# Thirteen Strassen pairs in the down-projection instead of twelve, placed one position earlier, with the order of the low parts changed

## What is computed

```python
def conv_glu_ffn(u, w_up, conv_ffn, b_conv_ffn, w_down):
    h = causal_dwconv(u @ w_up, conv_ffn) + b_conv_ffn
    return (jax.nn.silu(h[..., :D_FF]) * h[..., D_FF:]) @ w_down      # D_FF = 5632, result 256 x 2048

def hybrid_layer(x, ...):
    z = rms_norm(x, g_mix) @ w_in
    ...
    x = x + merged @ w_out
    x = x + cross_attend(rms_norm(x, g_cross), rms_norm(mem, g_mem), ...)
    x = x + conv_glu_ffn(rms_norm(x, g_ffn), w_up, conv_ffn, b_conv_ffn, w_down)
```

## Time and profile before

| | us |
|---|---|
| median of 3 runs (1742.89 to 1744.5) | 1743.65 |
| the profiled execution | 1744.25 |
| its span, first to last instruction | 1742.5 |
| PE busy in the span | 1732.3 |
| DVE busy | 1184.1 |
| ACT busy | 956.1 |

### The profile page before, as it was taken

How to read it: one execution, slowest core, us unless ns; L and a number is a source line. 1 busy time by engine, 2 the same in 40 slices (tenths; PEclk the granted TensorE clock), 3 DMA queues, 4 the chain that set the end, 5 groups by cost and what they waited for, 6 DMA issues and landing times.

```text
span 1742.5 us, 25685 instructions
## 1 busy us (share of the span) xinstructions
PE 1732.3 (99%) x8706; PEld 1470.0 (84%) x8706; DVE 1184.1 (68%) x1618; ACT 956.1 (55%) x1271; POOL 9.9 (1%) x22
## 2 busy tenths in 40 slices
PE   9999999999999999999999999999999999999999
PEld 7888888888788888888888888888888888888887
DVE  6788876667755455545565667777777666788777
ACT  7765656666754444444664565555555555555453
POOL 0000000000000000000000000000000000000000
PEclk9999999999999999999999999999999999999999
DMA  8555554476655555556855445555555555555654
GB/s 321 192 172 172 171 173 158 169 166 166 163 188 191 189 192 192 187 195 221 301 183 189 147 169 193 187 189 190 187 188 191 193 188 186 169 206 192 206 194 169
DMA packets 90960, 330.93 MB, mean 190 GB/s; under 512 B 10224, under 2 KB 10480, under 8 KB 89872
## 3 DMA queue, kind: packets, MB, share of 16 engines
q1 hardware_dynamic: 89424, 321.96, 54.7%
q0 software_dynamic: 1472, 8.12, 2.8%
HBM read 326.83 MB, written 2.10 MB: 189 GB/s over the span
## 4 chain that ended last, share of the span: by engine, by line
PE 93%; DVE 2%; DMA 2%; ACT 2%; issue 1%; SPq 0%; ACTq 0%; DVEq 0%
PE ps L381 22%; PE ps L362 13%; PE ps L364 13%; PE ps L363 13%; PE ps L384 11%; PE ps L756 4%; PE ps L758 4%; PE ps L757 4%; DMA w_raw<-in_stream 2%; PE ps L484 1%; PE ps L485 1%; PE ps L483 1%; PE ps L528 1%; PE ps L527 1%; ACT w_hi L843 1%
## 5 line engine op out<-in xcount | busy, mean ns | idle before, releaser
L1397 DVE TENSOR_TENSOR w_lo<-w_raw,w_hi 128x1024 fp32r<-128x1024 f32 x514 | 626.8, 1224 | 459.1 <-ACT w_hi L843 458.6
L843 ACT ACTIVATE w_hi<-w_raw 128x1024 fp32r<-128x1024 f32 x514 | 539.7, 1057 | 507.8 <-PE ps L364 309.7
L381 PE MATMUL ps<-u,w_hi 128*128 128x512 f32 x1664 | 580.8, 395 | 0.0
L384 PE MATMUL ps<-u,w_lo 128*128 128x256 f32 x1664 | 461.8, 278 | 0.0
L381 PEld LDWEIGHTS ps<-u,w_hi 128*128 128x128 f32 x1664 | 312.1, 188 | 72.4
L384 PEld LDWEIGHTS ps<-u,w_lo 128*128 128x128 f32 x1664 | 312.4, 188 | 0.2
L362 PE MATMUL ps<-w_hi,u 128*128 128x512 f32 x608 | 241.0, 396 | 0.6 <-DVE w_lo L1429 0.6
L364 PE MATMUL ps<-w_hi,u 128*128 128x512 f32 x608 | 237.4, 390 | 0.0
L363 PE MATMUL ps<-w_lo,u 128*128 128x512 f32 x608 | 237.0, 390 | 0.0
L362 PEld LDWEIGHTS ps<-w_hi,u 128*128 128x128 f32 x608 | 114.4, 188 | 24.6 <-issue 1.0
L364 PEld LDWEIGHTS ps<-w_hi,u 128*128 128x128 f32 x608 | 114.3, 188 | 24.2
(11 more groups left out here) (404 smaller groups left out, 2373.2 us busy)
## 6 DMA issues: line engine op xcount, KB each, us to landing
w_raw<-in_stream SPq DMA_DIRECT2D x600, 512.0 KB, 3.3
x_tok<-in_x SPq DMA_DIRECT2D x2, 1024.0 KB, 8.6
mem_raw<-in_mem_by_feature POOLq DMA_DIRECT2D x2, 1024.0 KB, 7.3
x_tok<-in_x POOLq DMA_DIRECT2D x2, 1024.0 KB, 7.6
mem_tok<-in_mem POOLq DMA_DIRECT2D x2, 1024.0 KB, 14.7
x_t<-in_x_t SPq DMA_DIRECT2D x7, 256.0 KB, 5.2
w_raw<-in_stream SPq DMA_DIRECT2D x4, 256.0 KB, 5.1
m_st<-ncm POOLq DMA_DIRECT2D x8, 128.0 KB, 9.4
```

The costliest lines, as they stand in the source:

```text
L381: pe.matmul(ps[:, bank + m, :], w_hi[:, s, lo:lo + P], act[:, kc, :, :].rearrange("p h t -> p (h t)"), start=(kc == 0), stop=False)
L384: mm = pe.matmul(ps[:, bank + m, T:2 * T], w_lo[:, s, lo:lo + P], act[:, kc, 0, :], start=False, stop=(kc == KC - 1))
L843: act.activation(w_hi[:, s, :], w_raw[:, s, :], ACT.Copy).then_inc(hi_made, 1)
L1397: TTo(w_lo[:, s, :], w_raw[:, s, :], w_hi[:, s, :].bitcast(F32), ALU.subtract).then_inc(lo_made, 1)
```

## The change

FAST_AT becomes a pair of tuples, one for each half: (3, 6, 9, 12, 15, 18) and (3, 6, 8, 11, 14, 16, 19). Half 1 thus has seven fast pairs, two of them (8 and 16) only two positions behind the fast pair ahead. The order of the pairs may differ between the halves, so the functions take the row pair q, not the position p. The seventh set of activation sums is made in one more iteration of the up loop that carries them. The activations of pair 2 are staged in the up pass (`h_hi_a` has room for three pairs), and in the down loops the stage of pair n+3 stands ahead of the split of pair n+2. The tail of the up pass moves from between the two chunks of a split to behind whole splits. In a fast pair's split on DVE, the low part of the blocks (`lo_made`) now stands ahead of the two `u_lo`. ACT's order inside a fast split is unchanged.

```diff
-FAST_AT = (4, 7, 10, 13, 16, 19)
+FAST_AT = ((3, 6, 9, 12, 15, 18), (3, 6, 8, 11, 14, 16, 19))
+FORMS = max(len(at) for at in FAST_AT)
...
-             ("h_hi_a", [P, 2, 2, T], F32R), ("dpad4", [P, 512 + 4096], F32), ("n_lo_a", [P, 4, BLK], F32R)])
+             ("h_hi_a", [P, 3, 2, T], F32R), ("dpad4", [P, 4096], F32), ("n_lo_a", [P, 4, BLK], F32R)])
...
             for n in range(2 * QN):
                 if n == 0:
                     up_low(UP_ITER - 1, 1, xb)
+                if n + 3 < QN:
+                    act.wait_ge(w_used, G_DOWN)
+                    stage(n + 3)
                 if n + 2 < 2 * QN:
                     down_split(n + 2)
-                if n + 2 < QN:
-                    act.wait_ge(w_used, G_DOWN)
-                    act.wait_ge(sem("h_made"), ORDER[n + 2] // 2 + 1 if n + 2 < 14 else UP_ITER)
-                    stage(n + 2)
...
+                if n == 0:
+                    up_first(UP_ITER - 1, 1, xb, ub)
...
                 TTo(u_sum[:, 3, :], u_sum[:, 2, :], b21, ALU.add).then_inc(sem("u_sums"), 1)
+                dve.wait_ge(hi_made, g + 2)
+                TTo(low[:, BLK:4 * BLK], raw[:, BLK:4 * BLK], high[:, BLK:4 * BLK].bitcast(F32), ALU.subtract
+                    ).then_inc(lo_made, 2)
                 dve.wait_ge(sem("u_sums"), 3 * i + 3)
                 for m in range(2):
                     dve.wait_ge(sem("u_high"), 2 * i + m + 1)
                     TTo(u_lo[:, 2 * m:2 * m + 2, :], u_sum[:, 2 * m:2 * m + 2, :],
                         u_hi[:, 2 * m:2 * m + 2, :].bitcast(F32), ALU.subtract).then_inc(sem("u_low"), 1)
-                dve.wait_ge(hi_made, g + 2)
-                TTo(low[:, BLK:4 * BLK], raw[:, BLK:4 * BLK], high[:, BLK:4 * BLK].bitcast(F32), ALU.subtract
-                    ).then_inc(lo_made, 2)
...
             for n in range(2 * QN):
                 if n == 0:
                     up_sum(UP_ITER - 1, 1, xb)
+                if n + 3 < QN:
+                    stage(n + 3)
                 if n + 2 < 2 * QN:
                     down_split(n + 2)
-                if n + 2 < QN:
-                    stage(n + 2)
-                if n % QN == FAST_AT[-1] + 1:
+                if n == 0:
+                    up_scale(UP_ITER - 1, 1, xb)
+                if n == 1:
+                    up_tap(1, UP_ITER - 1, 1, xb, ub)
+                    up_tap(0, UP_ITER - 1, 1, xb, ub)
+                if n == 2:
+                    up_gate(UP_ITER - 1)
+                if n % QN == FAST_AT[n // QN][-1] + 1:
```

More of the change, by code:

```diff
@@ L63, with _order @@
 QN = FC // 2
-FAST_AT = (4, 7, 10, 13, 16, 19)
-_fast = [2 * i for i in range(1, len(FAST_AT) + 1)]
-_plain = [q for q in range(QN) if q not in _fast]
-ORDER = [_fast.pop(0) if p in FAST_AT else _plain.pop(0) for p in range(QN)]
+FAST_AT = ((3, 6, 9, 12, 15, 18), (3, 6, 8, 11, 14, 16, 19))
+FORMS = max(len(at) for at in FAST_AT)
+def _order(at):
+    fast = [2 * i for i in range(1, len(at) + 1)]
+    plain = [q for q in range(QN) if q not in fast]
+    return [fast.pop(0) if p in at else plain.pop(0) for p in range(QN)]
+ORDER = [_order(at) for at in FAST_AT]
+FAST = [(j, p, ORDER[j][p] // 2 - 1) for j in range(2) for p in FAST_AT[j]]
 G_END = G_DOWN + FC * 2
@@ L215, in build, with h_high, h_pair @@
         STORES = [(bank, (bank % 4) // 2, (2 * (bank // 4) + bank % 2) * BLK) for bank in range(4, 8)]
[L217 to L222, removed]
+        def h_high(q):
+            p = ORDER[0].index(q)
+            home, first = (h_hi_a, 0) if p < 3 else (h_hi_b, 3) if p < 15 else (h_hi_c, 15)
             return home[:, p - first, :, :]
-        def h_pair(tensor, p):
-            return tensor[:, 2 * ORDER[p]:2 * ORDER[p] + 2, :]
+        def h_pair(tensor, q):
+            return tensor[:, 2 * q:2 * q + 2, :]
         def n_low(i):
@@ L758, in three, with down_products @@
                 return pe.matmul(o, a_lo, b_hi, start=False, stop=last)
-            def down_products(s, p, k, t, n, bank, first=False, last=False):
+            def down_products(s, q, k, t, n, bank, first=False, last=False):
                 rows, at = slice(t * P, (t + 1) * P), slice(n * BLK, (n + 1) * BLK)
-                return three(ps[:, bank, :], h_high(p, k)[:, rows], h_lo[:, 2 * ORDER[p] + k, rows],
+                return three(ps[:, bank, :], h_high(q)[:, k, rows], h_lo[:, 2 * q + k, rows],
                              w_hi[:, s, at], w_lo[:, s, at], first, last)
@@ L771, in down_plain @@
                         for n in range(2):
-                            mm = down_products((g + k) % SLOTS, p, k, t, n, 4 * j + 2 * t + n, first=(p == 0 and k == 0),
-                                               last=(j == 0 and p == QN - 1 and k == 1))
+                            mm = down_products((g + k) % SLOTS, ORDER[j][p], k, t, n, 4 * j + 2 * t + n,
+                                               first=(p == 0 and k == 0), last=(j == 0 and p == QN - 1 and k == 1))
                     mm.then_inc(w_used, 1)
             def down_fast(j, p):
-                g, i = G_DOWN + 2 * (QN * j + p), FAST_AT.index(p)
+                g, q = G_DOWN + 2 * (QN * j + p), ORDER[j][p]
+                i, done = q // 2 - 1, [(a, b) for a, b, c in FAST].index((j, p))
                 s0, s1 = g % SLOTS, (g + 1) % SLOTS
-                begin, end = i == 0, i == len(FAST_AT) - 1
+                begin, end = p == FAST_AT[j][0], p == FAST_AT[j][-1]
                 c11, c12, c21 = (ps[:, 4 * j + b, :] for b in range(3))
@@ L796, in down_fast @@
                 pe.wait_ge(lo_made, g + 2)
-                three(e1, h_high(p, 0)[:, early], h_lo[:, k1, early], *weights(s0, right), begin, end).then_inc(w_used, 1)
-                three(c11, h_high(p, 1)[:, early], h_lo[:, k2, early], *weights(s1, left), False, False)
+                three(e1, h_high(q)[:, 0, early], h_lo[:, k1, early], *weights(s0, right), begin, end).then_inc(w_used, 1)
+                three(c11, h_high(q)[:, 1, early], h_lo[:, k2, early], *weights(s1, left), False, False)
                 pe.wait_ge(sem("n_low"), i + 1)
                 three(c12, *form(N3), *weights(s1, right), False, False).then_inc(w_used, 1)
-                pe.wait_ge(sem("u_low"), 2 * (len(FAST_AT) * j + i) + 2)
+                pe.wait_ge(sem("u_low"), 2 * done + 2)
                 three(e5, *form(N5), *sums(0), begin, end)
@@ L804, in down_fast @@
                 three(e6, *form(N6), *sums(2), begin, end)
-                three(c21, h_high(p, 1)[:, late], h_lo[:, k2, late], *sums(3), False, False).then_inc(sem("fast_done"), 1)
+                three(c21, h_high(q)[:, 1, late], h_lo[:, k2, late], *sums(3), False, False).then_inc(sem("fast_done"), 1)
             for j in range(2):
@@ L1320, in stage @@
             def stage(p):
-                act.activation(h_high_pair(p), h_pair(h_ff, p), ACT.Copy).then_inc(sem("h_high"), 1)
+                q = ORDER[0][p]
+                act.wait_ge(sem("h_made"), q // 2 + 1 if p < 15 else UP_ITER)
+                act.activation(h_high(q), h_pair(h_ff, q), ACT.Copy).then_inc(sem("h_high"), 1)
             up_pass(Pos(G_UP), 0, True)
             up_pass(Pos(G_UP + UP_PER), 1, False)
-            act.wait_ge(sem("h_made"), 1)
             stage(0)
@@ L1346, in down_split @@
                         act.activation(w_hi[:, s + k, :], w_raw[:, s + k, :], ACT.Copy).then_inc(hi_made, 1)
-                        if n == 2 and k == 0:
-                            up_first(UP_ITER - 1, 1, xb, ub)
                     return
-                i = len(FAST_AT) * (n // QN) + FAST_AT.index(p)
+                i = [(a, b) for a, b, c in FAST].index((j, p))
                 if i:
@@ L2008, in _ @@
             i_home = 1
-            with dve.Fori(0, len(FAST_AT) - 4) as j:
+            with dve.Fori(0, FORMS - 4) as j:
                 up_pass(Pos(G_UP + 6 * UP_PER, j, UP_PER), j + 6, False, j + 4)
[L2011 to L2020, removed]
+            stage(2)
+            with dve.Fori(0, UP_ITER - 2 - FORMS) as j:
+                up_pass(Pos(G_UP + (2 + FORMS) * UP_PER, j, UP_PER), j + 2 + FORMS, False)
             def down_split(n):
-                g, p = G_DOWN + 2 * n, n % QN
+                g, j, p = G_DOWN + 2 * n, n // QN, n % QN
                 s = g % SLOTS
                 raw, high, low = (pair_slots(w, s) for w in (w_raw, w_hi, w_lo))
-                if p not in FAST_AT:
+                if p not in FAST_AT[j]:
                     for k in range(2):
@@ L2154, in lay_out @@
     for half in range(2):
-        for p, q in enumerate(ORDER):
+        for p, q in enumerate(ORDER[half]):
             pair = w_down[2 * q * P:(2 * q + 2) * P, 1024 * half:1024 * (half + 1)].reshape(2, P, 1024).copy()
-            if p in FAST_AT:
+            if p in FAST_AT[half]:
                 pair[0] = np.roll(pair[0], BLK, axis=1)
```

33 lines of the change are left out of this document (16 added, 17 removed).

## The result

The changed kernel takes 1758.68 us (1757.67 to 1760.09), against 1743.65 before: ratio 1.0088, 95% interval 1.0074 to 1.0101. It is slower by 15.0 us; 11.7 were forecast, in a range up to 1759.5, so the time lies 0.8 us inside it.

A forecast was written before the change was run, and what follows sets the result against it. PE was taken as the bound (busy 1732.3 of 1742.5 us), so matmuls and gaps count. Terms -0.7 + 2.9 + 1.1 + 1.1 + 4.2 + 2.0 + 1.1 = +11.7 on 1743.65 gave 1755.3 us, range 1749.3 to 1759.5.

The forecast's parts named there:

- gaps feed each other: Rival, 9%: u_lo behind lo_made delays low parts, refill and next S; steps 16.3 us, three clock falls, +17.6, 1761 us.
- Thirteenth pair: One more fast pair, in half 1: three matmuls fewer at 0.2267 us each, -0.7 us.
- Start: Down pass up to pair 6 of half 0: pair 2's gap goes, PE idles 3.3 us before pair 3; +2.9 us.
- Rest of half 0: Pairs 9, 12, 15, 18: 15.9 us steps against PE's 15.64, less gaps removed; +1.1 us, bounds -0.9 and +2.5.
- Half 1, pair 3: Its S waits behind adding half 0's result; lo_made at +17.1, PE arrives at 16.3; +1.1 us.
- Pairs 8 and 16: Half 1: sums wait for fast_done of pairs 6 and 14; 1.9 us idle, 0.2 around it, twice; +4.2 us.
- the clock: PE's clock falls after gaps of 1.7 to 1.9 us; one loss taken net, +1.1 us, bounds 0 and 4.8.
- Pairs 6, 11, 14, 19: Half 1: no slack, as in half 0, 0.5 us each; +2.0 us, bounds 0 and +3.
- The clock against the rule: By the skill's rule planned gaps keep the clock up, sum 1.1 us lower; the trace disagreed, so the term stayed.

The follow-up runs named there:

- The filler: The changed kernel with u_lo ahead of the blocks' low part, plus an unread VectorE reduction of about 2.2 us directly behind that low part in each fast split: 1759.31 us.
- the run with `up_first` late: The changed kernel with ScalarE's up_first of the last up iteration moved behind the stage of pair 4 instead of ahead of it: 1756.19 us.
- the twelve pairs: The changed kernel with fast pairs (3, 6, 9, 12, 15, 18) in both halves: 1758.27 us; with u_lo also ahead of the low part again: 1745.55 us.

## Why the prediction was right, and where it missed

The direction and the range held, and so did most of the mechanism: what the start of the first sum waits for, `lo_made` at + 7.0 us, and the gaps at the close pairs. For the rest of half 0 it did not hold: what happened there is what the rival "gaps feed each other" describes. The 1758.68 us measured are 3.4 above the forecast and 2.3 below that rival's 1761, so the run looks as much like the one as like the other. By its own steps, against the profile after:

- *Thirteenth pair, -0.7.* Three matmuls fewer; right.
- *Start, +2.9.* The first sum came 12.5 us into the pass, as worked out, the gap was 3.1 us idle for 3.3, and pair 6 started 39.6 us in (39.4 forecast), 3.1 us later than before; with pair 6 itself it is +3.4. That PE's clock costs nothing there holds too: it was down for 6 us of that stretch (0.53) and PE still waited 1.43 us at pair 6.
- *Rest of half 0, +1.1.* It was +3.6 (4.5 against 0.9), above the bound of +2.5 that I had given it. This is the step that failed. I took the steps of VectorE from the earlier trace rows as they were, 15.9 us, and let PE pay what goes beyond 15.64. But those steps were made with `u_lo` inside the wait for ScalarE; the change puts 2.3 us behind `lo_made`, and the step grew to 16.7 to 16.9. At each of the four pairs that is 0.6 to 0.8 us of idling, where I had 0.3, and 0.4 us of restart and `u_low`, where I had 0.2. I had named this feedback as a rival, at 9%, and argued that what refills late is a queue released by `lo_made`, which does not move. But two of the four chunks, those of the next fast pair, are released by the low parts of the plain pair behind `u_lo`, and these do move. The filler showed VectorE's time there to be the cause: 16.7 to 17.0 us with it, 15.1 to 16.2 without.
- *Half 1, pair 3, +1.1.* 1.3; right.
- *Pairs 8 and 16, +4.2, and the clock, +1.1.* Together 7.5: the idle time and the restart were 2.1 us each, as forecast, and the clock fell behind both, where I had one loss partly made good. *Pairs 6, 11, 14, 19, +2.0.* 0.6. These terms are one account, which I kept as three. In the run with `up_first` late the clock did not fall behind 8 and 16; there pairs 8 and 16 had 4.7 us and 11, 14 and 19 had 2.4, together 7.2 us. In the changed kernel they had 7.5 and nothing. A slow clock that makes PE late gives VectorE time, and what it cost in all was 0.3 us. The four runs with `up_first` late say the same: they lie within 0.2 us of each other, at mean granted clocks of 0.998 to 1.000. Where VectorE keeps up, a slow clock is not free: of the five runs with `u_lo` first, the one at 1.000 took 1749.9 us and the four at 0.997 to 0.998 took 1751.2 to 1751.9. The sum of the three terms, 7.3, against 8.1 with pair 6, was about right.
- *The clock against the rule.* The clock fell behind idle times of 1.83 us: 0.66 of full was granted from 1674.5 to 1678.5 and 0.57 from 1720 to 1724. The Trainium skill ("TensorE: Matmul & The Clock Gate", section "HAM oscillation — how this bites in real kernels") has the rule that idle gaps below a certain length, which these are, do not lower it; these two disagree (rows in the last section). The term that the rule would have struck out was there in the profile, but worth next to nothing in the total.

The total is 15.6 in the profile, and 2.5 us of the 3.9 missed lie in the rest of half 0. The others, 0.5 at the start, 0.2 at pair 3 and 0.8 in the account of half 1, are misses of size.

My expectations for the twelve pairs and for the positions of before missed for two reasons: I priced each gap by itself, though VectorE's step was the bound in every one, and I did not follow the taps through the new order.

## What to carry to other kernels

Where two engines make one thing in turn, an order changed on one of them moves nothing until the other's is changed with it: here each alone cost 7 to 11 us, and both together gave 10. When work leaves a wait in which it was hidden, price it by what stands behind it, down to the slots that it frees and the transfer that refills them, and compare the engine's whole period, from one such round to the next, with that of the engine that bounds the kernel. Gaps of a bound engine that is fed by a slower loop are one account: taking one away, or a slow clock that fills it, brings it back at the next.

## What the runs showed of the hardware

The same idle time of PE was followed by a slow clock in one run and not in another. After 3.10 us the clock was 0.53 in the stretch of the changed kernel and 1.00 in the run with twelve pairs and `u_lo` first. After 1.83 us it was 0.66 and 0.57 in stretches of 4 us behind the two gaps of the changed kernel, and 1.00 behind both in the run with `up_first` late. So in these runs the length of a gap between 1.8 and 3.1 us does not settle by itself whether the clock falls.

The stretch behind pair 16 of half 1 in the changed kernel and in the run with `up_first` late:

```profile
1720.00:1724.00 4.00, 4.00 (x12) 3.18 (x11) 4.00 (x4) 0.88 (x1) 0.00 (x0) 0.57 0.72 262
```

```profile
1718.10:1722.10 4.00, 4.00 (x17) 3.04 (x18) 4.00 (x4) 0.58 (x1) 0.00 (x0) 1.00 0.72 259
```

In 4 us PE starts 12 matmuls at the lower clock and 17 at the full one.
